# Hybrid streaming encoder step on one core: Vector's output steps, rotary key and key steps placed behind copies of the triangular inverse

## The reference

```python
proj = rmsnorm(xf, norm_mix_g) @ w_in                 # 2208 columns
c = rmsnorm(p_mla[..., 256:384]); kr = rope(rmsnorm(p_mla[..., 384:416]), pos)
ql = rmsnorm(p_mla[..., :256]); q = ql @ w_q_up       # queries; keys and values from c @ w_kv_up
xm = p_rw + (shifted - p_rw) * mu_shift               # token-shift mix: r, k, v and three low-rank inputs
kk = k * k_k / norm; k_eff = k * (1 + (a - 1) * k_a)
# group B, per head and token (delta rule):
S = S * w + (S @ -kk) (kk * a)^T + v k^T;  y = S @ r
yn = (y - mean) * rsqrt(var + eps) * lnx_g + lnx_b
out = (yn + bonus) * (sigmoid(gl) @ g2)               # "output steps" below
```

## Time and profile before

| | us |
|---|---|
| median of three runs | 1930.74 (1929.92 to 1931.53) |
| the profiled execution | 1930.67 |
| its span, first to last instruction | 1928.9 |
| mean granted clock of TensorE | 0.977 of full |
| TensorE busy | 1812.8 (94% of the span) |
| Vector busy | 1011.0 (52%) |
| GpSimd busy | 690.5 (36%) |
| Scalar busy | 368.5 (19%) |

### The profile page before, as it was taken

One profiled execution on the slowest core, in us unless ns is written; L12 is line 12 of the kernel. 1 busy time (PEld: TensorE's weight loads), 2 busy tenths in 40 slices (PEclk: granted clock), 3 DMA queues, 4 the chain that ended last, 5 costly groups with the idle time before them and its releaser, 6 DMA issues. The chain is left out here.

```text
span 1928.9 us, 34297 instructions
## 1 busy us (share of the span) xinstructions
PE 1812.8 (94%) x14597; PEld 1353.1 (70%) x14597; DVE 1011.0 (52%) x1746; ACT 368.5 (19%) x918; POOL 690.5 (36%) x495
## 2 busy tenths in 40 slices
PE   4999999999998896999999899999999999899998
PEld 3566666666665664555556688888888888688887
DVE  1777777778767785455343543444334334414422
ACT  2332332333233221333400201110000110000000
POOL 2564464464454453444520022222221120543522
PEclk8999999999998897999999999999999999999999
DMA  8343143243232004210040211111111111233331
GB/s 333 115 149 101 56 154 101 64 146 102 70 129 56 24 13 110 95 45 1 1 188 12 90 44 44 44 44 44 44 44 44 44 44 53 90 124 108 126 98 64
DMA packets 70761, 157.12 MB, mean 81 GB/s; under 512 B 19273, under 2 KB 47769, under 8 KB 66514
## 3 DMA queue, kind: packets, MB, share of 16 engines
q1 hardware_dynamic: 66722, 114.23, 18.4%
q10 hardware_dynamic: 3888, 40.70, 5.9%
HBM read 126.80 MB, written 20.44 MB: 76 GB/s over the span
## 5 line engine op out<-in xcount | busy, mean ns | idle before, releaser
L2304 PE MATMUL psum<-mixT,wA 128*128 128x264 f32 x1408 | 337.3, 388 | 1.9 <-DVE rb L2546 1.5
L412 PE MATMUL psum<-wsl,xt 128*128 128x368 f32 (+1 forms) x1156 | 290.8, 458 | 12.9 <-DMA wsl<-in_w_in 9.7
L2304 PEld LDWEIGHTS psum<-mixT,wA 128*128 128x128 f32 x1408 | 268.4, 191 | 48.6 <-DVE rb L2546 1.7
L2304 PE MATMUL psum<-u_sum,wA 128*128 128x264 f32 x1232 | 297.4, 386 | 0.5 <-DVE u_sum L2529 0.5
L2304 PEld LDWEIGHTS psum<-u_sum,wA 128*128 128x128 f32 x1232 | 234.4, 190 | 41.0 <-issue 0.9
L412 PEld LDWEIGHTS psum<-wsl,xt 128*128 128x128 f32 (+1 forms) x1156 | 155.4, 173 | 96.4 <-issue 21.2
L2459 POOL TENSOR_TENSOR wA<-wA 128x512 f32<-128x512 f32 x22 | 29.0, 1316 | 427.2 <-DMA wA<-in_w_gate 229.1
L2304 PE MATMUL psum<-hid,wA 128*128 128x264 f32 x528 | 121.5, 386 | 2.1 <-DVE hid L2597 1.5
L2304 PEld LDWEIGHTS psum<-hid,wA 128*128 128x128 f32 x528 | 100.2, 190 | 19.9 <-issue 2.8
L2304 PE MATMUL psum<-mixT,u_sum 128*128 128x264 f32 x352 | 82.9, 393 | 9.4 <-POOL u_sum L2478 9.2
L2472 POOL TENSOR_TENSOR u_sum<-wA 128x1280 f32<-128x1280 f32 x8 | 25.1, 3140 | 184.0 <-DMA wA<-in_w_down 184.0
(11 more groups left out here) (363 smaller groups left out, 2933.1 us busy)
## 6 DMA issues: line engine op xcount, KB each, us to landing
wsl<-in_w_in ACTq DMA_DIRECT2D x27, 1472.0 KB, 6.9
wA<-in_w_down SPq DMA_DIRECT2D x32, 704.0 KB, 4.1
wA<-in_w_gate SPq DMA_DIRECT2D x22, 512.0 KB, 4.3
wA<-in_w_up SPq DMA_DIRECT2D x22, 512.0 KB, 4.4
mixed<-proj SPq DMA_DIRECT2D x8, 784.0 KB
xt<-in_x_tiles SPq DMA_DIRECT2D x9, 512.0 KB, 4.1
wsl<-in_w_in SPq DMA_DIRECT2D x3, 1472.0 KB, 13.2
out_y<-hid SPq DMA_DIRECT2D x1, 4224.0 KB, 12.0
```

Source lines behind the costliest of these rows:

```text
L412: return pe.matmul(out, lhsT, rhs, start=start, stop=stop)
L2304: ins = pe.matmul(pb[bank][:, 0:NW], left(k), right(k), start=first and k == 0, stop=k == depth - 1, skip_group_check=not first)
```

## The change

Four moves in lists that are written out by hand; no operation is added or removed.

1. Vector: `y_out(t - 1)` moves from before `lats(f)` to behind the first level's `level_d(t, 0)`, just ahead of `level_t(t, 1)`.
2. TensorE: `transposes_rw(t - 1)` moves from before to behind `level_ed(t, 1)`. Scalar: `rw_out(t - 1)` moves from before `lora_in(f)` to behind `e_out(t, 1)`.
3. Vector: `level_t(t, 1)` goes ahead of `rope_key(f)`.
4. Vector: `level_t(t, 4)` goes ahead of `key_mods(f)`.

```diff
             transposes_lat(f)
             level_t(t, 1)
-            if t:
-                transposes_rw(t - 1)
             F(2)
...
             level_ed(t, 1)
+            if t:
+                transposes_rw(t - 1)
...
             latents(f)
-            if t:
-                rw_out(t - 1)
...
             e_out(t, 1)
+            if t:
+                rw_out(t - 1)
...
             lat_means(f)
-            if t:
-                y_out(t - 1)
             lats(f)
             level_d(t, 0)
             sample_scores(t, 1)
-            rope_key(f)
+            if t:
+                y_out(t - 1)
             level_t(t, 1)
             sample_scores(t, 2)
+            rope_key(f)
             mix_lora(f)
...
             level_d(t, 3)
             sample_scores(t, 7)
-            key_mods(f)
             level_t(t, 4)
             sample_scores(t, 8)
+            key_mods(f)
             keys(f)
```

## The result

| | before | after |
|---|---|---|
| median of the runs, us | 1931.13 (1929.92 to 1933.16) | 1953.80 (1950.94 to 1959.16) |
| ratio, 95% interval | | 1.0129 (1.0110 to 1.0147) |
| profiled execution, us (its span) | 1930.67 (1928.9) | 1952.72 (1950.9) |
| mean granted clock | 0.977 | 0.970 |
| TensorE, Vector, GpSimd busy, us | 1812.8, 1011.0, 690.5 | 1824.7, 1006.8, 693.7 |

The forecast was 1941.9 us with a range up to 1949. The direction was right and the size was not: 22.7 us between the medians, where the sum said 11.2. TensorE is busy 11.9 us longer with the same 14,597 products. That alone says that part of the loss is not waiting: the same work runs slower. The two medians alone give a ratio of 1.0117, inside the interval. One of the twelve executions of the last kernel of this document, 2156.82 us at a granted clock of 0.84, is left out of its numbers.

A forecast was written before the change was run, and what follows sets the result against it. TensorE, nearly solid in nine token tiles, was taken as the bound, with only its waits to win. Terms 2.0 - 0.1 + 1.0 + 6.4 + 0.1 - 0.4 + 2.2 = +11.2 us on 1930.67 gave 1941.9 us, range 1933 to 1949.

The forecast's parts named there:

- Part two: Level five's T1 ahead of the key steps: Vector idles, queries come late, +1.06 us a tile in tiles 0 to 5.
- Part one: Latents before output steps, T1 before rotary key: +0.4 us in tiles 1 to 4 and 6, -0.1 tile 5, +1.0 tile 0.
- rival 3: TensorE's clock falls behind the new wait before the queries: seven tiles, +14 to +25, 1956 to 1967 us; chance 0.07.
- the two cases: The forecast sum of 1941.9 us without a clock fall, and the clock falling in seven tiles, 1956 to 1967 us.
- Tile 8: Last tile, sample attention: output steps (2.9 us) ahead of T1h delay the second level's products, +2.2 us.
- Small terms: Tile 0 +2.06 us, tile 6 +0.5, tile 7 -0.4; attention and the tail unchanged.

The follow-up runs named there:

- the last kernel of this document: Changed kernel with GpSimd's receptance mixes behind the key norms, key steps split, both filling pieces ahead of the queries' transposes: 1920.62 us, 0.9951 of the kernel before.
- The first experiment: The kernel before with one move alone, T1 of level five ahead of the key steps: 1942.21 us, ratio 1.0068.
- the split: Changed kernel with the first two of the four key steps put back ahead of level five's T1: 1935.55 us, 1.0037 of the kernel before.
- the experiment's tile: Tile 8 of the changed kernel with that tile's output steps, their transposes and output projection in the old order: 1952.36 us, 1.0112 of the kernel before.
- the kernel meant for it: The kernel before with Vector's first multiply of the keys done five times more in tiles 0 to 7: 1941.05 us, ratio 1.0040.

## Why the prediction was right and where it was wrong

- **Part two was right, by its own steps.** Vector idles 1.46 us before the fifth T1h (1.4 forecast), the 0.81 us wait goes, the last query step falls one GpSimd operation earlier, and the queries start 1.12 us late (1.06). The wait is 2.44 us (2 to 2.5). The first experiment puts it at 1.0 to 1.2 us in tiles 0, 1 and 3, and 0.7 in tile 5, where the clock holds, and the split shows that the idle time causes it.
- **Part one was right in two tiles, and had the right sum from two wrong sizes in four.** The latents idle and collide as said (0.96 and 1.31 us), and L483 leaves 0.45 us late (0.4). In tiles 1 and 2 all of it came: two collisions for the output steps, one for the rotary key, T1h 1.6 us earlier, a wait of 0.41 us for it (0.45) and of 1.47 us before L483 (1 to 1.5). In tiles 3 to 6 the output steps took three collisions and the key none. So T1h came 0.66 us earlier in tile 3, the wait for it fell to 1.35 us only, and the one before L483 is 0.56 us. That the sum is the same is no luck: one collision moved from the key to the output steps, and both stand ahead of L483.
- **The step that failed is the price of the clock: nothing in the sum, and rival 3 at a chance of 0.07.** The evidence against it was that waits of 1.62 us leave tile 3 at full clock, although my own forecast made a wait of 2.3 us, longer than any in the earlier trace rows. The clock fell behind this wait in four of the six tiles that have it (0 to 5): TensorE is busy 1.6 to 1.7 us more in each of tiles 1, 3, 4 and 5 than in tile 2, 6.5 of the 10.7 us that the tiles' sum lacks. It was less than rival 3's "seven tiles" and its 2 us each; by the prediction's own rows only six tiles have the late queries, and no row gives its upper end of 25 us. So the result lies between the two cases, and the range should have reached to 1960. The Trainium skill (TensorE: Matmul & The Clock Gate, "Part 1: The HAM clock gate") says that the number of slow products at a kernel's start varies from run to run with the phase of the gate. No run here shows the phase; the trace has the same kind of scatter, 1.7 us lost in tile 3 and none in tile 2 behind the same 2.4 us.
- **Tile 8 was sized at +2.2 and cost 4.6, another 2.4 of the 10.7.** The forecast left out the clock there too. One output step met a mask (L1616, 1.46 us), Vector idled 1.84 us as forecast (1.7), the wait became 3.54 us, and at half clock TensorE is busy 1.4 us more there (27.55 against 26.18 in the experiment's tile).
- **Small terms.** Tiles 0, 6 and 7 came out 0.3 to 0.4 us above their forecast. Attention and the tail were forecast at no change; what lies behind the last T1h took 2.3 us longer, with TensorE busy 2.6 us more (1188.93 against 1186.29), and tile 0 started 2.2 us earlier in the profiled execution. In the kernels profiled here that last part takes 1231 to 1236 us whatever the change, so this is put down to no move.

Still open: why the clock falls behind one 2.44 us wait and not behind the next, how much of tile 7's time is the kernel's, and what a wait of that length does with no step moved, since the kernel meant for it fell short.

## What to carry to other kernels

When a forecast creates a wait on an engine whose clock can fall, compare its length with the longest wait that the trace shows at full clock, and if it is longer, price the fall as the main case, not as a tail. Before moving an urgent step ahead of others, check that its input is there by then: here the copy moved ahead could run no sooner than its producer, and the time that the passed steps had filled was lost; splitting them so that just enough stays in front recovered it. Where two engines take turns on memory, look for the order on the other engine: moving GpSimd's mixes away won 12 us by the medians, while moving Vector's steps among them only changed which of them paid.

## What was not expected of the hardware

- Collisions hold both engines. Beside Vector's output steps the mixes of GpSimd take 1.60 us instead of 1.27, and Vector's steps 1.64 instead of 0.69, in turn. In such a row Vector goes at GpSimd's pace: L1616, L1618 and L1620 start 1.67 and 1.68 us apart in tile 3, and L1224 and L1225 start 1.67 us apart.
- The query steps stand beside GpSimd in the same way: 0.9 and 2.3 us of extra work on Vector both made the queries 1.3 us late.
- Half clock against the longest wait in a tile, over tiles 1 to 6 of fourteen profiled executions: behind waits of 3.6 to 3.7 us it fell in 6 of 6 tiles, behind 2.44 in 11 of 15, behind 2.12 in 2 of 2, and with no wait over 2.03 us in 0 of 61. In tile 0 it held behind 2.44 or 2.45 us in all three kernels that have that wait, so 11 of 18 there. These are counts from this kernel and no rule. Each fall in the changed kernel cost 1.6 to 1.7 us.
